# Head-centred values and initial states in a bidirectional RWKV step: the mean of the chunk norm leaves the latent scans

## The chip, the cores and the metric

One core of a Trainium2 chip. The metric is the device time of one execution of the whole kernel in microseconds (us), as the median of several runs. Engines: TensorE (PE; its weight loads, PEld, are recorded apart), VectorE (DVE), ScalarE (ACT), GpSimd (POOL), and SyncE (SP), which issues DMAs.

## The reference, cut to what matters

One layer of a bidirectional hybrid backbone on 1024 latent and 128 context tokens, model width 1024. A projection `z = xn @ w_in` gives receptances, keys, values and gates. Sixteen heads of 64 run an RWKV-7 recurrence forward and backward, the outputs of both directions are added, and each head's output is normalised over its 64 value dimensions:

```python
def step(S, inp):
    r_t, w_t, k_t, v_t, a_t, b_t = inp
    sa = jnp.einsum('bhvk,bhk->bhv', S, a_t)
    S = S * w_t[:, :, None, :] + sa[..., None] * b_t[:, :, None, :] + v_t[..., None] * k_t[:, :, None, :]
    return S, jnp.einsum('bhvk,bhk->bhv', S, r_t)
...
wkv = ys[0] + ys[1]
mu = jnp.mean(wkv, axis=-1, keepdims=True)
var = jnp.mean(jnp.square(wkv - mu), axis=-1, keepdims=True)
ln = ((wkv - mu) * lax.rsqrt(var + LNX_EPS)).reshape(B, T, D_RWKV) * p['lnx_w'] + p['lnx_b']
```

The output is linear in the values `v` and the initial state `S0` along the value dimension. So if each token's `v` and each column of `S0` have zero mean over the 64 value dimensions of a head, `wkv` has it too, and `mu` is zero. The final states of the context scan are an output of their own and must not be centred. The bonus term uses the uncentred `v`. Around the recurrence stand a gated short convolution, an output projection and a squared-ReLU MLP.

## The kernel before, in words

Heads are worked on in 8 pairs (128 rows: two heads of 64). The kernel has three stages.

**Projections** (the dense loop over `p` in every engine's function). For each pair TensorE fills PSUM banks in a fixed order, held by the class `Fills` (L104): first the low-rank products `w0, w1, a0, a1`, then `AFTER` (L99): `k, r, v, ks, cc, ch, vt, cb, g, za, bon, zb`. Each name is three fills of 384 tokens (`g` is six: for each third of the tokens one bank per head). Eight banks go round: fill n uses the bank of fill n - 8 and waits until that was emptied (`Fills.freed`, `free_bank`). `BY_DVE` (L101) names the fills that VectorE empties (`ch`, `cb`, `bon`); ScalarE empties the others. `vt` is the transpose of the values (`vf`) to token-major form; ScalarE copies it to `vn` (L1616), from where SP stores it to `v_d` (L674). VectorE's order in a pair is: decay sums, the substitution for the pair before, key scaling, the operands, then the product of `ch` with `cc` (L2071), the convolution (L2076 to L2083), the eviction of `cb` (L2088) and that of `bon` (L2093). `g` is the diagonal product of TensorE (`diagonal`, L1075), which asks for both of its banks before each third. ScalarE rounds a weight block for the high part (`split_high`), POOL forms the low part (L847), and SP loads blocks four ahead into a ring.

**Scans.** 72 units: for each pair, chunks j = 0 to 7 of 128 latent tokens (forward chunk j together with backward chunk 7 - j) and one context chunk (j = 8), which starts from a zero state. Step s of each engine's loop holds a fixed list of work for several units in flight: TensorE turns and inverts (`turn`, `left`, `right`), forms the grams of unit s + 4 and does the serial products of unit s (`ur_state`, `serial_ur`, `serial_u`, `serial_s`, `serial_y`). ScalarE moves `ur` (L1651) and `up` (L1655) to SBUF; VectorE masks the grams (L2108), updates the states (L2157), and adds the second half of `y` (L2168) for j = 4 to 7, ScalarE the first half for the other j. `first_state(p)` (L2129) makes a pair's initial states by two products at the step j = 8 of the pair before. One chunk is finished in each step from s = 5 on (`finals`, L177): TensorE takes the head sums of `y` with a block of ones (`mean`, L1296), VectorE subtracts (`centred`, L2180), ScalarE squares (L1675), TensorE sums the squares (`variance`) and forms the gate product (`gate`), ScalarE takes the root, VectorE the reciprocal (L2184), TensorE spreads it, and VectorE scales (`scaled`, L2189 to L2196). 67 chunks are finished in the loop and five in a tail behind it (`TAIL`, L187).

**Dense stage.** Output projections and MLP as 11 products of 7 block products each (L1411), not touched.

Of the kernel before, what the change touches and what calls it, by code (L numbers as in the profile page):

```python
# [22 lines left out]
P = 128  # L23
# [4 lines left out]
G = 3  # L28
# [69 lines left out]
LOW_RANK = [(x + str(d), cg) for x in "wa" for cg in range(G) for d in range(2)]  # L98
AFTER = ["k", "r", "v", "ks", "cc", "ch", "vt", "cb", "g", "za", "bon", "zb"]  # L99
DIAGONAL = [(f"g{h}", cg) for cg in range(G) for h in range(2)]  # L100
BY_DVE = ("ch", "cb", "bon")  # L101


class Fills:  # L104
# [59 lines left out]
def y_seen(u):  # L164

    p, j = divmod(u, NC)
    if y_by_act(j):
        return "ya_ok", 5 * p + (j + 1 if j < NC_LAT else 5)
    return "yd_ok", 4 * p + j - 3
# [7 lines left out]
def finals(s):  # L177

    p, j = divmod(s, NC)
    if s < 0 or s >= UNITS:  # L180
        return []
    if j > 4:
        return [(p, FIN_ORDER[j - 5], NC * p + j - 5)]
    return [(p - 1, FIN_ORDER[4 + j], NC * (p - 1) + 4 + j)] if p else []
# [88 lines left out]
def flow_step(nc, xs, xp, wblocks, wquads, pack, packl, vecs, csil_in, consts, gfin, y_out, yp_out, st_out):  # L273
    ctx = ExitStack()
    with ctx:
# [20 lines left out]
        def sb(st, name, shape, dt=F32):  # L296
            return st.enter_context(nc.sbuf_tensor(name, shape, dt))
# [41 lines left out]
        pk = sb(dense, "pk", [P, PK])  # L339
        half = sb(dense, "half", [P, 6])  # L340
        mid = sb(dense, "mid", [P, 2, NC])
        dense.close()
        rounded = ExitStack()
        sb(rounded, "under_cv", [P, (KT + 5) * T])
# [44 lines left out]
        state = [[sb(sc, f"state{d}{q}", [P, HD]) for q in range(2)] for d in range(2)]  # L389
        mrow = sb(sc, "mrow", [P, MG])  # L390
        fstd = sb(sc, "fstd", [P, 5, 2])
        fbon, fsq = (sb(sc, n, [P, 5, C]) for n in ("fbon", "fsq"))
        tok = [sb(sc, f"tok{q}", [P, 2, 4, HD]) for q in range(TOKS)]
        pl = [sb(sc, f"pl{q}", [P, PL]) for q in range(2)]
# [573 lines left out]
        def _(pe):  # L968
# [325 lines left out]
                return banks[(0, 4, 2)[k] + i // 4][:, (i % 4) * P:(i % 4 + 1) * P]  # L1294

            def mean(p, c, n):  # L1296
                name, seen = y_seen(NC * p + (max(c, NC_LAT - 1 - c) if c < NC_LAT else NC_LAT))
                pe.wait_ge(S[name], seen)
                if 0 < n < TAIL[0][2]:
                    pe.wait_ge(S["xa_ok"], n)  # L1300
                for hs in halves_of:
                    ins = mm(place(n, 0)[hs, :], bones[hs, hs], yf[p % 2][hs, c * C:(c + 1) * C], True, True)
                ins.then_inc(S["mu_full"], 1)
# [18 lines left out]

            def gate(p, c, n):
                pe.wait_ge(S[f"pl_in{p % 2}"], 16 * (p // 2 + 1))
                if n < TAIL[0][2]:
                    pe.wait_ge(S["yc_ok"], n + 1)
                for b in halves_of:
                    ins = mm(place(n, 2)[b, :], pl[p % 2][:, PL_G2 + b.start:PL_G2 + b.stop], gl[:, c * C:(c + 1) * C], True, True)
                ins.then_inc(S["gate_full"], 1)
# [7 lines left out]
            def modulation_turned(g):  # L1337
                pe.wait_ge(S["mrow_ok"], g + 1)
                if g:
                    pe.wait_ge(S["yc_ok"], finals(NC * g + 3)[0][2] + 1)  # L1340
                for b in range(4):
                    ins = mm(banks[2][:, 3 * P + 2 * b:3 * P + 2 * b + 2], mrow[:, b * P:(b + 1) * P], sel[:], True, True)
                ins.then_inc(S["mt_full"], 1)
# [144 lines left out]
        def _(act):  # L1488
# [41 lines left out]
            def empty(p, name, out, func, **kw):  # L1530
                for cg in range(G):
                    act.wait_ge(S["fill_full"], FL.full(p, name, cg))
                    A(out(cg), banks[FL.bank(p, name, cg)][:, :GN], func, **kw).then_inc(ev["A"], 1)
# [33 lines left out]
            for p in range(PAIRS):  # L1567
                act.wait_ge(S["half_ok"], p + 1)
                for kind in "wa":
                    if p:  # L1570
                        for d in range(2):
                            act.wait_ge(S[f"so_{'ar0' if kind == 'w' else 'bk0'}{d}"], 16 * p)
                    for name, cg in LOW_RANK:
                        if name[0] == kind:
                            d = int(name[1])
                            dst = (ar0 if kind == "w" else bk0)[d]
                            b = d if kind == "w" else 2 + d
                            act.wait_ge(S["fill_full"], FL.full(p, name, cg))
                            A(dst[:, cols(cg)], banks[FL.bank(p, name, cg)][:, :GN], ACT.Tanh, scale=0.5, bias=half[:, b:b + 1]).then_inc(ev["A"], 1)
                for d in range(2):  # L1580
                    own(p, f"w{d}")
                    A(ar0[d][:], ar0[d][:], ACT.Copy, scale=-0.5 * DECAY, bias=-0.5 * DECAY).then_inc(S["logw_ok"], 1)
                if p:
                    act.wait_ge(S["op_ok"], 8 * p)
                    act.wait_ge(S["prod_ok"], p)
                    act.wait_ge(S["g_out"], 32 * p)
                empty(p, "k", lambda cg: kt[:, cols(cg)], ACT.Copy)
                next_split(p, "k")
                own(p, "k")
                A(kd[1][:], kt[:], ACT.Square, scale=pk[:, PK_VEC + V_KK:PK_VEC + V_KK + 1]).then_inc(S["kksq_ok"], 1)  # L1590
                act.wait_ge(S["kksq_ok"], p + 1)
                if p:
                    act.wait_ge(S["gb_out"], 16 * p)
                A(cv_r[:], kd[1][:], ACT.Copy).then_inc(S["parts_ok"], 1)
                k_factor(p, 0)
                decays(p, 0)
                empty(p, "r", lambda cg: rt[:, cols(cg)], ACT.Copy)
                next_split(p, "r")
                decays(p, 1)
                if p:  # L1600
                    act.wait_ge(S["so_f"], 16 * p)
                empty(p, "v", lambda cg: vf[:, cols(cg)], ACT.Copy)
                next_split(p, "v")
                if p:
                    act.wait_ge(S["inv_ok"], p)
                empty(p, "ks", lambda cg: kk[:, cols(cg)], ACT.Sqrt)
                k_factor(p, 1)
                if p:
                    act.wait_ge(S["ga_out"], 16 * p)
                empty(p, "cc", lambda cg: cct[:, cols(cg)], ACT.Copy)  # L1610
                next_split(p, "cc")
                next_split(p, "ch")
                if p:
                    act.wait_ge(S["so_v"], 16 * p)
                    act.wait_ge(S["x_out"], 64 * Q * p)
                empty(p, "vt", lambda cg: vn[:, cols(cg)], ACT.Copy)  # L1616
                next_split(p, "cb")
                act.wait_ge(S["prod_ok"], p + 1)
                A(kd_r[1][:], kd[0][:], ACT.Copy).then_inc(S["parts_ok"], 1)
                for name, cg in DIAGONAL:  # L1620
                    act.wait_ge(S["fill_full"], FL.full(p, name, cg))
                    A((kt, rt)[int(name[1])][:, cols(cg)], banks[FL.bank(p, name, cg)][:, :GN], ACT.Copy).then_inc(ev["A"], 1)
                act.wait_ge(S["conv_ok"], p + 1)
                empty(p, "za", lambda cg: cct[:, cols(cg)], ACT.Tanh, scale=0.5)
                next_split(p, "za")
                act.wait_ge(S["xb_out"], 16 * p + 16)
                empty(p, "zb", lambda cg: cv[:, cols(cg)], ACT.Tanh, scale=0.5)
                next_split(p, "zb")
# [42 lines left out]
                return banks[2][:, 4 * P - 2:4 * P] if i < 0 else ser[:, 1, 2 * i:2 * i + 2]  # L1671

            def squares_of(p, c, n):
                act.wait_ge(S["yc_ok"], n + 1)
                A(fsq[:, n % 5, :], yf[p % 2][:, c * C:(c + 1) * C], ACT.Square).then_inc(S["ysq_ok"], 1)  # L1675

            def deviation(p, c, n):
# [193 lines left out]
        def _(dve):  # L1871
# [141 lines left out]
            def substitution(p, some=range(SUB - 1), ways=(0, 1)):  # L2013
# [9 lines left out]
                for x in some:  # L2023
# [8 lines left out]
                    for d in ways:  # L2032
# [6 lines left out]
                        else:  # L2039
                            ch.step(ins)  # L2040
                            done[d] = ch.n

            halves(0)
            dve.wait_ge(ev["A"], FL.emptied("l", 2)[1])
            V.tensor_scalar(gl[:], gl[:], 0.5, 0.5, mul, add).then_inc(S["gl_ok"], 1)
            for p in range(PAIRS):
# [22 lines left out]
                for cg in range(G):  # L2069
                    x = full(p, "ch", cg)  # L2070
                    V.tensor_tensor(cct[:, cols(cg)], x, cct[:, cols(cg)], mul).then_inc(ev["D"], 1)  # L2071
                filled(p, "ch")
                if p:
                    dve.wait_ge(S["gb_out"], 16 * p)
# [53 lines left out]

            def first_state(p):  # L2129
                dve.wait_ge(S[f"pl_in{p % 2}"], 16 * (p // 2 + 1))  # L2130
                for d in range(2):
                    c = chunk(d, 0)
                    V.tensor_scalar(state[d][0][:], pl[p % 2][:, PL_ST + d * HD:PL_ST + (d + 1) * HD], emid[:, p, d, c:c + 1], None, mul).then_inc(S["s_ok"], 1)

            def carried(u):

# [38 lines left out]
                return banks[(0, 4, 2)[k] + i // 4][:, (i % 4) * P:(i % 4 + 1) * P]  # L2175

            def centred(p, c, n):
                dve.wait_ge(S["mu_full"], n + 1)
                y = yf[p % 2][:, c * C:(c + 1) * C]
                stt(y, place(n, 0), -1.0 / HD, y, mul, add).then_inc(S["yc_ok"], 1)  # L2180

# [52 lines left out]
            for x in finals(UNITS - 1):  # L2234
                reciprocal(*x)
                scaled(*x)
            dve.wait_ge(S["mu_full"], UNITS)
            for x in TAIL:
                centred(*x)
            for x in TAIL:  # L2240
# [324 lines left out]
```

## Time and profile before

| | |
|---|---|
| median of 3 runs | 2705.92 us (2702.68 to 2709.07) |
| the profiled execution | 2705.67 us, of which the span from first to last instruction is 2703.6 us |
| mean granted clock of TensorE | 0.985 of full speed |
| TensorE busy | 2580.1 us (95%) |
| VectorE busy | 1852.0 us (68%) |
| ScalarE busy | 1080.2 us (40%) |
| POOL busy | 1175.8 us (43%) |

Projections last from about 100 to 1020 us of the span, the scans to about 1640 us. Times in the rows are microseconds from the start of the span unless they are marked ns. A row of the timeline has start, length, engine, line, operation and tiles (out<-in), and in brackets the time for which the engine stood before it and what ended that time. Busy shares are averages over stages; L970 is a helper through which nearly all matmuls are issued, so they are told apart by their tiles.

### The profile page before, as it was taken

How to read it: one execution, taken by the hardware profiler on the slowest of the kernel's cores; microseconds unless marked ns; L12 is line 12 of the kernel's file. 1: busy time of each engine (PE TensorE's matmuls, PEld its weight loads, DVE VectorE, ACT ScalarE, POOL GpSimd, SP SyncE). 2: the span in 40 equal slices, each digit the busy share in tenths (PEclk: the TensorE clock that was granted, in tenths of full speed). 3: DMA queues.
4: the chain of work that ended last, by engine and by line, in shares of the span. 5: the costliest groups of instructions: out<-in, count | busy, mean ns of one | idle time of the engine just before them, and what ended most of it. 6: DMA issues, size and time to landing. Idle time of an engine off the chain costs nothing.

```text
span 2703.6 us, 68164 instructions
## 1 busy us (share of the span) xinstructions
PE 2580.1 (95%) x28864; PEld 2430.1 (90%) x28864; DVE 1852.0 (68%) x3010; ACT 1080.2 (40%) x1978; POOL 1175.8 (43%) x1154
## 2 busy tenths in 40 slices
PE   4899999999999998999999997999799999999998
PEld 3899999999999996788878887999799999999998
DVE  3464665846748464787766666799778679678686
ACT  3434243342433422433333343443453353443534
POOL 1323222322223224555555544656446556565662
PEclk8999999999999999999999999999899999999999
DMA  8333425435254363444454456454223232333231
GB/s 323 106 110 109 144 69 181 125 97 158 62 174 128 94 193 108 131 143 144 138 154 137 139 160 195 131 175 105 63 63 79 81 101 70 79 84 102 65 79 71
DMA packets 282412, 329.15 MB, mean 122 GB/s; under 512 B 76288, under 2 KB 215936, under 8 KB 273536
## 3 DMA queue, kind: packets, MB, share of 16 engines
q1 hardware_dynamic: 274448, 278.66, 33.2%
q0 software_dynamic: 5904, 39.32, 6.9%
q10 hardware_dynamic: 1760, 6.82, 0.6%
q8 instruction: 231, 3.78, 0.6%
q14 instruction: 69, 0.57, 0.1%
HBM read 221.83 MB, written 91.36 MB: 116 GB/s over the span
## 4 chain that ended last, share of the span: by engine, by line
PE 85%; DVE 7%; issue 2%; DMA 2%; ACT 2%; SPq 1%; POOL 0%; DVEq 0%; ACTq 0%; POOLq 0%
PE ser L970 18%; PE gbank L970 13%; PE bank L970 11%; PE inv L970 11%; PE gbank L1411 8%; PE inv L1411 8%; PE ser L1411 7%; PE bank L1411 7%; DVE a_sum L2298 1%; DMA ring<-in_wblocks 1%; PE inv L1172 1%; PE bank L1155 1%; DVE a_sum L2302 1%; DVE a_sum L2306 1%; DVE a_lo L2272 1%
## 5 line engine op out<-in xcount | busy, mean ns | idle before, releaser
L952 POOL TENSOR_TENSOR w_lo<-raw_w,w_hi 128x512 fp32r<-128x512 f32 x264 | 425.3, 1624 | 370.2 <-ACT w_hi L1747 370.1
L847 POOL TENSOR_TENSOR wsp<-ring,wsp 128x1024 fp32r<-128x1024 f32 x67 | 210.8, 3146 | 670.7 <-ACT wsp L1513 670.7
L1747 ACT ACTIVATE w_hi<-raw_w 128x512 fp32r<-128x512 f32 x264 | 165.1, 632 | 262.5 <-PE ser L1411 98.4
L970 PE MATMUL ser<-xn_hi,wsp 128*128 128x384 f32 x816 | 217.7, 340 | 6.1 <-POOL xn_lo L853 6.1
L1411 PE MATMUL gbank<-a_hi,w_hi 128*128 128x288 f32 x616 | 185.7, 302 | 30.6 <-POOL w_lo L952 14.6
L970 PE MATMUL gbank<-xn_hi,wsp 128*128 128x384 f32 x800 | 213.0, 339 | 1.1 <-issue 1.1
L970 PE MATMUL bank<-xn_hi,wsp 128*128 128x384 f32 x800 | 211.1, 338 | 2.2 <-POOL wsp L847 2.2
L970 PE MATMUL inv<-xn_hi,wsp 128*128 128x384 f32 x800 | 211.3, 338 | 0.5 <-issue 0.5
L2108 DVE TENSOR_TENSOR gmat<-gbank,gmask 128x1024 f32<-128x1024 f32 x144 | 175.6, 1219 | 49.8 <-PE gbank L970 49.0
L1733 ACT ACTIVATE a_hi<-a_sum 128x1152 fp32r<-128x1152 f32 x88 | 103.1, 1173 | 224.6 <-DVE a_sum L2306 78.0
L970 PE MATMUL gbank<-ub 64*64 64x128 f32 (+1 forms) x3456 | 178.4, 310 | 9.5 <-DVE gmat L2108 5.6
L1411 PE MATMUL gbank<-a_hi,w_lo 128*128 128x288 f32 x616 | 184.7, 300 | 0.0
L1411 PE MATMUL gbank<-a_lo,w_hi 128*128 128x288 f32 x616 | 184.4, 299 | 0.0
L1411 PE MATMUL inv<-a_hi,w_lo 128*128 128x288 f32 x616 | 183.9, 299 | 0.0
L1411 PE MATMUL inv<-a_hi,w_hi 128*128 128x288 f32 x616 | 183.7, 298 | 0.0
L1411 PE MATMUL inv<-a_lo,w_hi 128*128 128x288 f32 x616 | 183.6, 298 | 0.0
L1411 PE MATMUL ser<-a_hi,w_hi 128*128 128x288 f32 x616 | 181.6, 295 | 1.5 <-ACT r L1786 1.5
L1411 PE MATMUL bank<-a_hi,w_lo 128*128 128x288 f32 x616 | 181.8, 295 | 0.0
L1411 PE MATMUL ser<-a_hi,w_lo 128*128 128x288 f32 x616 | 181.7, 295 | 0.0
L1411 PE MATMUL ser<-a_lo,w_hi 128*128 128x288 f32 x616 | 181.4, 294 | 0.0
L1411 PE MATMUL bank<-a_lo,w_hi 128*128 128x288 f32 x616 | 181.4, 294 | 0.0
L1411 PE MATMUL bank<-a_hi,w_hi 128*128 128x288 f32 x616 | 181.3, 294 | 0.0
(398 smaller groups left out, 7534.7 us busy)
## 6 DMA issues: line engine op xcount, KB each, us to landing
ring<-in_wblocks SPq DMA_DIRECT2D x107, 512.0 KB, 4.8
ub<-op_d SPq DMA_DIRECT2D x144, 256.0 KB, 2.8
raw_w<-in_wquads SPq DMA_DIRECT2D x33, 1024.0 KB, 4.8
raw_w<-in_wquads POOLq DMA_DIRECT2D x22, 1024.0 KB, 8.8
op_d<-ar SPq DMA_DIRECT2D x32, 576.0 KB, 5.4
op_d<-bk SPq DMA_DIRECT2D x32, 576.0 KB, 6.2
raw_w<-in_wquads SPq DMA_DIRECT2D x44, 256.0 KB, 3.3
raw_w<-zsum POOLq DMA_DIRECT2D x11, 1024.0 KB, 12.3
```

The costliest lines, as they stand in the source:

```text
L847: GT(wsp[s % 2][1][:], ring[(N_ADA_RING + s) % RING][:], wsp[s % 2][0][:].bitcast(F32), ALU.subtract).then_inc(S["wsplit_lo"], 1)
L952: GT(w_lo[n % 4][:], src, w_hi[n % 4][:].bitcast(F32), ALU.subtract).then_inc(S["wl_ok"], 1)
L970: return nc.tensor.matmul(out, lhsT, rhs, start=start, stop=stop)
L1155: ins = nc.tensor.transpose(banks[3][:, y * P:(y + 1) * P], ub[v % LOADS][:, y // 2, 2 + y % 2, :], ident[:])
L1172: ins = nc.tensor.transpose(inv[:, 0, x * P:(x + 1) * P], xt[:, place_of(v), :, :].rearrange("p h t -> p (h t)"), ident[:])
L1411: return nc.tensor.matmul(out, lhsT, rhs, start=start, stop=stop, skip_group_check=True)
L1733: A(a_hi[:, places2(q, j), :], src, ACT.Copy).then_inc(S["ah_ok"], 1)
L1747: A(w_hi[s][:], raw_of(op)[:, m, :].rearrange("p (k c) -> p k c", k=KH), ACT.Copy).then_inc(S["wh_ok"], 1)
L2108: V.tensor_tensor(gmat[v % SETS][:, d, :, :, :].rearrange("p h x t -> p h (x t)"), gbank[:, :, :], gmask[:, d:d + 1, :].to_broadcast([P, 2 ...
L2272: V.tensor_tensor(a_lo[:, places2(q, j), :], src, a_hi[:, places2(q, j), :].bitcast(F32), sub).then_inc(S["al_ok"], 1)
L2298: ch.step(V.tensor_tensor(o[j], a11[j], a12[j], sub))
L2302: ch.step(V.tensor_tensor(o[j], o[j], a22[j], add))
```

## The change

The values leave the projection stage centred per head for the latent tokens, the initial latent states are centred, and the scans skip the mean product and the subtraction for latent chunks. Context chunks keep both. The waits on the centred output are moved to what now comes last (`y_seen`, `xa_ok`).

```diff
-BY_DVE = ("ch", "cb", "bon")
+BY_DVE = ("ch", "vt", "cb", "bon")
...
+        vmean = sb(dense, "vmean", [P, G, 2 * G])
+        smean = sb(sc, "smean", [P, 2])
...
             def mean(p, c, n):
-                name, seen = y_seen(NC * p + (max(c, NC_LAT - 1 - c) if c < NC_LAT else NC_LAT))
-                pe.wait_ge(S[name], seen)
+                if c == NC_LAT:
+                    name, seen = y_seen(NC * p + NC_LAT)
+                    pe.wait_ge(S[name], seen)
                 if 0 < n < TAIL[0][2]:
                     pe.wait_ge(S["xa_ok"], n)
+                if c < NC_LAT:
+                    return
...
             def gate(p, c, n):
                 pe.wait_ge(S[f"pl_in{p % 2}"], 16 * (p // 2 + 1))
-                if n < TAIL[0][2]:
-                    pe.wait_ge(S["yc_ok"], n + 1)
+                if n < TAIL[0][2] and c == NC_LAT:
+                    pe.wait_ge(S["yc_ok"], p + 1)
...
                 if g:
-                    pe.wait_ge(S["yc_ok"], finals(NC * g + 3)[0][2] + 1)
+                    pe.wait_ge(S["xa_ok"], finals(NC * g + 3)[0][2])
...
                 next_split(p, "ch")
-                if p:
-                    act.wait_ge(S["so_v"], 16 * p)
-                    act.wait_ge(S["x_out"], 64 * Q * p)
-                empty(p, "vt", lambda cg: vn[:, cols(cg)], ACT.Copy)
                 next_split(p, "cb")
...
             def squares_of(p, c, n):
-                act.wait_ge(S["yc_ok"], n + 1)
+                if c < NC_LAT:
+                    name, seen = y_seen(NC * p + max(c, NC_LAT - 1 - c))
+                    act.wait_ge(S[name], seen)
+                else:
+                    act.wait_ge(S["yc_ok"], p + 1)
...
+            def value_tokens(p):
+
+                n = [2 * G] * (G - 1) + [2 * G - 2]
+                for cg in range(G):
+                    x = full(p, "vt", cg).rearrange("p (g v) -> p g v", v=HD)
+                    ch.step(V.tensor_reduce(vmean[:, cg, 0:n[cg]], x[:, 0:n[cg], :], mybir.AxisListType.X, add))
+                ch.settle()
+                if p:
+                    dve.wait_ge(S["so_v"], 16 * p)
+                    dve.wait_ge(S["x_out"], 64 * Q * p)
+                for cg in range(G):
+                    x = full(p, "vt", cg).rearrange("p (g v) -> p g v", v=HD)
+                    stt(vn[:, cols(cg)].rearrange("p (g v) -> p g v", v=HD), bc(vmean[:, cg, :], HD), -1.0 / HD, x, mul, add).then_inc(ev["D"], 1)
...
                     V.tensor_tensor(cct[:, cols(cg)], x, cct[:, cols(cg)], mul).then_inc(ev["D"], 1)
+                value_tokens(p)
                 filled(p, "ch")
...
             def first_state(p):
                 dve.wait_ge(S[f"pl_in{p % 2}"], 16 * (p // 2 + 1))
+                s0 = pl[p % 2][:, PL_ST:PL_ST + 2 * HD]
+                ch.step(V.tensor_reduce(smean[:], s0.rearrange("p (d v) -> p d v", v=HD), mybir.AxisListType.X, add))
+                ch.settle()
+                ch.step(V.tensor_scalar(smean[:], smean[:], -1.0 / HD, None, mul))
+                ch.settle()
                 for d in range(2):
                     c = chunk(d, 0)
-                    V.tensor_scalar(state[d][0][:], pl[p % 2][:, PL_ST + d * HD:PL_ST + (d + 1) * HD], emid[:, p, d, c:c + 1], None, mul).then_inc(S["s_ok"], 1)
+                    V.tensor_scalar(state[d][0][:], s0[:, d * HD:(d + 1) * HD], smean[:, d:d + 1], emid[:, p, d, c:c + 1], add, mul).then_inc(S["s_ok"], 1)
...
             def centred(p, c, n):
-                dve.wait_ge(S["mu_full"], n + 1)
+                if c < NC_LAT:
+                    return
+                dve.wait_ge(S["mu_full"], p + 1)
```

## Rows read from the trace of the kernel before

**Rows 1.** Windows of projections and scans: length; busy PE, PEld, DVE, ACT, POOL; PEclk, DMA.

```profile
300.00:500.00 200.00, 200.00 (x1396) 194.83 (x1395) 115.66 (x232) 83.12 (x128) 58.11 (x19) 1.00 0.42 128
1200.00:1300.00 100.00, 99.81 (x2471) 80.90 (x2468) 72.20 (x176) 38.41 (x105) 50.97 (x110) 1.00 0.45 134
```

**Rows 2.** The page's chain that ended last, shares by engine.

```profile
PE 85%; DVE 7%; issue 2%; DMA 2%; ACT 2%; SPq 1%; POOL 0%; DVEq 0%; ACTq 0%; POOLq 0%
```

**Rows 3.** Groups by line: busy us, mean ns of one | idle before, releaser.

```profile
L970 PE MATMUL bank<-yf,bones 64*64 64x128 f32 x268 | 26.8, 270 | 1.4 <-DVE yf L2196 0.9 <-issue 0.5
...
L2180 DVE SCALAR_TENSOR_TENSOR yf<-bank,yf 128x128 f32<-128x128 f32 x67 | 19.5, 291 | 14.2 <-PE bank L970 13.0
...
L2184 DVE RECIPROCAL fstd<-fstd 128x2 f32<-128x2 f32 x72 | 11.4, 159 | 15.0 <-ACT fstd L1681 14.9
```

**Rows 4.** Timeline of two scan steps, weight loads, and ScalarE in the second.

```profile
1045.22 0.55 PEld L970 LDWEIGHTS ser<-ur,tt 128*64 128x64 f32 x16 [0.17 <-issue]
1046.78 0.20 PEld L970 LDWEIGHTS ser<-up,tok 128*64 128x64 f32 x4 [0.39 <-ACT up L1655]
...
1242.86 0.55 PEld L970 LDWEIGHTS ser<-ur,tt 128*64 128x64 f32 x16 [0.17 <-issue]
...
1244.63 0.20 PEld L970 LDWEIGHTS ser<-up,tok 128*64 128x64 f32 x4 [0.17 <-issue]
...
1243.59 0.38 ACT L1655 ACTIVATE up<-ser 128x256 f32<-128x256 f32 x1 [0.98 <-PE ser L970]
```

**Rows 5.** Timeline of VectorE in one pair's projections.

```profile
418.51 1.02 DVE L2071 TENSOR_TENSOR cct<-gbank,cct 128x384 f32<-128x384 f32 x2
419.44 0.55 DVE L2071 TENSOR_TENSOR cct<-bank,cct 128x384 f32<-128x384 f32 x1
420.02 0.82 DVE L2076 TENSOR_SCALAR cv<-cct,pk 128x1152 f32<-128x1152 f32 x1
...
424.07 1.02 DVE L2088 TENSOR_TENSOR cv<-ser,cv 128x384 f32<-128x384 f32 x2
```

**Rows 6.** Timeline of the weight loads in the same pair.

```profile
419.11 0.19 PEld L970 LDWEIGHTS gbank<-xn_hi,wsp 128*128 128x128 f32 x1 [0.28 <-DVE cct L2071]
...
424.88 0.14 PEld L970 LDWEIGHTS ser<-ar,bk 64*64 64x64 f32 x2
```

**Rows 7.** Timeline of SyncE's DMA queue in the same pair.

```profile
379.89 5.78 SPq L626 DMA_DIRECT2D x_d<-vn  x15
...
418.42 1.25 SPq L674 DMA_DIRECT2D v_d<-vn  x1
```

**Rows 8.** Timeline at a pair boundary of the scans, VectorE and weight loads.

```profile
1261.32 1.22 DVE L2108 TENSOR_TENSOR gmat<-gbank,gmask 128x1024 f32<-128x1024 f32 x1
...
1264.65 0.21 PEld L970 LDWEIGHTS inv<-xtb,gmat 64*64 64x64 f32 x8 [0.17 <-POOL lm L878]
```

**Rows 9.** Gaps of TensorE: timeline, windows (PE busy, PEclk, DMA), last-ending chain.

```profile
1904.96 0.19 PEld L1411 LDWEIGHTS gbank<-a_hi,w_hi 128*128 128x128 f32 x1 [1.85 <-DVE r L2377]
...
1906.00:1908.00 2.00, 2.00 (x18) 1.00 0.59 201
...
1702.08 0.19 PEld L1411 LDWEIGHTS gbank<-a_hi,w_hi 128*128 128x128 f32 x1 [3.19 <-ACT r L1761]
...
1704.00:1706.00 2.00, 2.00 (x10) 0.50 0.00 0
...
1702.11 4.95 PE gbank L1411 x24
1707.05 3.18 PE bank L1411 x24
...
1040.67 1.16 PEld L970 LDWEIGHTS gbank<-ub 64*64 64x64 f32 x24 [2.27 <-DMA vb<-v_d]
...
1305.60 0.65 PEld L970 LDWEIGHTS gbank<-ub 64*64 64x64 f32 x24
```

**Rows 10.** Timeline of the weight loads, a step with j = 7.

```profile
1247.42 0.32 PEld L970 LDWEIGHTS ser<-state,ub 64*64 64x64 f32 x16 [0.27 <-DVE yf L2168]
```

More of the change, by code:

```diff
@@ L2041, in substitution @@
                             done[d] = ch.n
+            def value_tokens(p):
[10 more added lines that the diff above has]
+                    stt(vn[:, cols(cg)].rearrange("p (g v) -> p g v", v=HD), bc(vmean[:, cg, :], HD), -1.0 / HD, x, mul, add).then_inc(ev["D"], 1)
             halves(0)
+            ch.step(V.memset(vmean[:, G - 1, 2 * G - 2:2 * G], 0.0))
             dve.wait_ge(ev["A"], FL.emptied("l", 2)[1])
@@ L2236, in _ @@
                 scaled(*x)
-            dve.wait_ge(S["mu_full"], UNITS)
+            dve.wait_ge(S["mu_full"], PAIRS)
             for x in TAIL:
```

## The prediction

> **What bounds the kernel now.** I read the windows by stage first, to see which engine is full in which stage [rows 1]: TensorE is busy for all 200 of 200 us in the projections and for 99.8 of 100 us in the scans, VectorE for 58% and 72%. The chain that ended last agrees [rows 2]: 85% of the span is TensorE. So VectorE and ScalarE count only where TensorE waits for them, and a busy TensorE record may still hide a wait (matmul ends are modelled); therefore the places themselves are read in the timeline of TensorE's weight loads, which shows when its queue stands.
>
> **Part 1, removed: the mean product of 64 latent chunks.** Sixty lie inside the scans (67 chunks are finished in the loop, seven of them context chunks, which keep it), four in the tail. The product's group is 26.8 us busy for 67 chunks, 0.40 us each, and the centring 0.29 us on VectorE [rows 3]. But what a step gains is read from two steps that differ by just this [rows 4]: with the mean, 1.77 us pass from the first weight load of `serial_u` (1242.86) to that of `serial_s` (1244.63); in pair 0, where no chunk is being finished yet, 1.56 us (1045.22 to 1046.78). The difference is 0.21 us, half the busy time, because the matmuls of the gram before it still fill the array. `serial_s` also waits for ScalarE's `up`, which ends at 1243.97 (1243.59 + 0.38), 1.11 us after `serial_u` began: it stays just off the path. Gain 60 x 0.21 = 12.6 us. Bounds: 0, and 60 x 0.40 = 24 us. The centring on VectorE is worth nothing: the states behind it wait for TensorE. The four tail chunks save at most 4 x 0.29 = 1.2 us and are taken at nothing; the gates there wait for an earlier chunk's last VectorE step. The square on ScalarE may start earlier, which nobody waits for.
>
> **Part 2, moved: the token-major values go from ScalarE (3 copies a pair, on an engine 42% busy: worth nothing) to VectorE as 3 reductions, a wait for them, and 3 subtractions.** Queued behind them on VectorE are the convolution and then the eviction of `cb`; and the eviction of `cb`'s first group is what TensorE waits for. Eight PSUM banks go round: the third group of the diagonal product `g` takes the bank of the first group of `cb` (fill 14 of the list against fill 6). How tight this is shows in one pair [rows 5]: VectorE evicts `ch` from 418.51 to 419.99, starts the convolution at 420.02 and the `cb` evictions at 424.07, so the first is done at 424.62 (0.55 us). TensorE begins the third group of `g` at 424.88 [rows 6]: 0.26 us of slack. The same kind of wait exists already: TensorE stood 0.28 us for the first `ch` eviction (ended 419.06, load at 419.11, so 0.05 us for the signal).
>
> The added work: instructions on 128x384 PSUM follow each other every 0.47 us ((419.44 - 418.51)/2) [rows 5]. From 419.91 on: two reductions at 0.47, the third (256 elements) at its full 0.41 (0.55 less 128 elements at the 1.0 ns that lie between the 384-element row [rows 5] and the 128-element one [rows 3]), 0.04 for the wait, three subtractions at 0.47: the convolution starts at 422.71 instead of 420.02, 2.69 us later. The first `cb` bank is free at 427.31, plus 0.05 for the signal: TensorE starts the third group at 427.36 instead of 424.88, a stall of 2.48 us. Nothing gives it back: TensorE is full before and behind, and VectorE's next work in the pair is anchored to TensorE's fills. 8 x 2.48 = 19.8 us lost. No row shows a reduction. If it cost nothing, the stall would be 2.48 - 1.25 = 1.2 us (9.8 us in all; some of the wait stays); if it ran at half the rate, 3.84 us (30.7 us). I take the rate of the nearest row, the `ch` eviction.
>
> The Trainium skill, page "VectorE: DVE Perf Modes", section "The DRAIN you can't avoid", says that a VectorE instruction starts only when the pipe of the one before it is empty. The `ch` evictions here overlap by 0.08 us, so the trace disagrees; by the rule the six would take about 3.2 us and the loss would be 24 us instead of 19.8. Its "Rules for kernel authors" call `tensor_reduce` the slowest VectorE instruction, with one element per cycle: a rule against this change, which no row here shows.
>
> The waits for the older `v_d` and `x_d` transfers now stand on VectorE; the last `x_d` store is issued by 385.7, 35 us before, and `v_d` a pair before [rows 7], so they cost nothing. SP waits for the `vt` eviction, so the `v_d` store (418.42) goes out some 4.3 us later, and with it the weight load queued behind it; `xb_d`, `pk` and `g_d` go some 2.7 us later. The weight ring is loaded four blocks ahead, and the queue is idle between; without this cover the 4.3 us would stand once a pair.
>
> **Part 3, added: the centred initial state.** At seven pair boundaries VectorE does a reduction over 128 elements, a two-element scale and two waits: 0.29 [rows 3] + 0.16 + 2 x 0.04 = 0.53 us, before the mask of the next gram (1261.32) [rows 8]. Behind that mask are POOL's `lm` (0.17 us waited for at 1264.65) and the next gram. With some 0.13 us of slack: 7 x 0.4 = 2.8 us lost. Bounds 0 and 3.7.
>
> **Part 4, the clock.** A stop of 2.5 us may cost more than itself. A gap of 1.85 us in dense work left the granted clock at 1.00; a gap of 3.19 us was followed by 0.50 (1.2 GHz), and the group of 24 matmuls behind it took 4.95 instead of 3.18 us; a gap of 2.27 us in sparse work (1040.67) lies on the same side, since the loads behind it took 1.16 us where the same 24 take 0.65 [rows 9]. So one fall costs 1.77 us; between 0 and 8 of the new stops (0 to 14.2 us) cause one. The new gap lies between the rows, about half-way; I take three, 5.3 us. The Trainium skill, page "TensorE: Matmul & The Clock Gate", section "What's actually happening", says that the throttled state is the default and that activity releases it; that makes a new stop a candidate each time, and by it alone the time would be the dear case below.
>
> **The sum.** -12.6 + 19.8 + 2.8 + 5.3 = +15.3 us. The profiled execution took 2705.7 us (span 2703.6), the median of three runs is 2705.9; so 2721 us. A measurement of this kernel can tell about 0.2% (5.4 us) from no change.
>
> **Rivals.**
> - Faster, about 2696 us. A scan step is set by VectorE's chain and not by TensorE, so that the removed centring takes with it the 0.27 us for which TensorE waits for VectorE's `yf` [rows 10] in the four last latent steps of a pair (32 x 0.27 = 8.6 us), besides the full 0.40 us (24 us). 32.6 against 19.8 + 2.8 gives -10 us. It decides from 0.47 us a chunk on ((22.6 + 5.4)/60). For it: TensorE does wait there. Against it: [rows 4] have the step without a mean, and it is 0.21 shorter. Chance 0.09.
> - No difference, about 2706 us. The reductions cost next to nothing and no clock falls: 9.8 + 2.8 - 12.6 = 0. For it: no reduction is in the trace; against it: 384 elements are read however it is done. Chance 0.14.
> - The dear case, about 2731 us. The clock falls at all or nearly all eight stops: 2721 - 5.3 + 14.2 = 2730, with a slower reduction more. Chance 0.15.
> - The forecast: a stall of 2 to 3 us in each pair, with up to five falls of the clock, 2711 to 2726 us. Chance 0.62.
> That the mean isn't really removed can be left out: the diff returns before its matmuls.
>
> **How the numbers follow.** The likeliest is 2721. The range goes from 2707 to 2731: from the upper part of the no-difference case, over the forecast, to the dear case without its tail. Slower by over 0.2%: 0.62 + 0.15 = 0.77; within 0.2%: 0.14; faster: 0.09.
>
> **What would show it.** In the projections: three reductions and three subtractions between the evictions of `ch` and the convolution, about 2.7 us together; a gap of about 2.5 us in the weight loads before the third group of `g`, released by VectorE's `cv`, eight times; a granted clock of 0.50 behind some of them. A pair should last 2.5 us and more longer. In the scans: a step shorter by 0.21 us, with 1.56 us from `serial_u` to `serial_s`; a pair of nine steps shorter by about 1.7 us less 0.4 at its boundary. I am wrong if TensorE has no such gap, if the gap is under 1.2 us, or if a step shrinks by 0.4 us or more.

## The result, and the profile after

| | before | after |
|---|---|---|
| median of 4 runs each, same chip | 2706.19 us (2702.68 to 2709.07) | 2755.26 us (2750.86 to 2758.60) |
| span of the profiled execution | 2703.6 us | 2756.6 us |
| mean granted clock | 0.985 | 0.976 |
| up to the first scan step (ScalarE's first `ur`) | 1043.75 us | 1106.07 us |
| from there to the last of the 72 steps | 580.20 us | 572.38 us |
| behind it | 1079.65 us | 1078.15 us |

The changed kernel is 1.8% slower: ratio 1.0181, 95% interval 1.0160 to 1.0202. The forecast was 2721 us, its range ended at 2731: the direction was right, the size was not. The last three lines of the table, each worked out from the timeline of ScalarE, say where the time went: +62.3 us in the projections, -7.8 in the scans, -1.5 behind them. The scans gave 7.8 of the 9.8 us that were forecast; the projections lost two and a half times the forecast (19.8 + 5.3 = 25.1 us).

The windows answer to [rows 1] (same columns). TensorE, full in 200 of 200 us before, now is busy for 187; the scans hardly differ.

```profile
300.00:500.00 200.00, 186.83 (x1303) 181.31 (x1302) 120.79 (x187) 67.72 (x103) 49.36 (x16) 0.97 0.44 133
1200.00:1300.00 100.00, 99.20 (x2453) 79.65 (x2449) 80.48 (x204) 38.30 (x105) 51.74 (x111) 1.00 0.47 139
```

The waits of the weight loads between 100 and 1060 us (total, times, longest) name the loss. There are eight stops, two on each of four banks, 53.4 us in all, each 6.7 us long. All are released by VectorE's `cv`, as forecast; the forecast length was 2.48 us.

```profile
PEld inv L972 <- DVE cv L2109: 13.4, 2, 6.7
PEld gbank L972 <- DVE cv L2109: 13.4, 2, 6.7
PEld bank L972 <- DVE cv L2109: 13.3, 2, 6.7
PEld ser L972 <- DVE cv L2109: 13.3, 2, 6.7
```

Why 6.7 is read from VectorE's timeline of one pair (it answers to [rows 5]):

```profile
435.86 1.02 DVE L2091 TENSOR_TENSOR cct<-gbank,cct 128x384 f32<-128x384 f32 x2
436.79 0.55 DVE L2091 TENSOR_TENSOR cct<-bank,cct 128x384 f32<-128x384 f32 x1
437.26 0.55 DVE L2053 TENSOR_REDUCE vmean<-bank 128x6 f32<-128x384 f32 x1
437.72 0.88 DVE L2053 TENSOR_REDUCE vmean<-inv 128x6 f32<-128x384 f32 x2
438.63 0.55 DVE L2060 SCALAR_TENSOR_TENSOR vn<-vmean,bank 128x384 f32<-128x384 f32 x1
439.11 1.01 DVE L2060 SCALAR_TENSOR_TENSOR vn<-vmean,inv 128x384 f32<-128x384 f32 x2
440.03 0.81 DVE L2097 TENSOR_SCALAR cv<-cct,pk 128x1152 f32<-128x1152 f32 x1
440.88 1.53 DVE L2100 SCALAR_TENSOR_TENSOR cv<-cct,pk,cv 128x1008 f32<-128x1008 f32 x2
442.45 3.24 DVE L2103 SCALAR_TENSOR_TENSOR cv<-cct,pk,cv 128x1008 f32<-128x1008 f32 x1
445.61 2.69 DVE L2104 SCALAR_TENSOR_TENSOR cv<-cct,pk,cv 128x127 f32<-128x127 f32 x1
448.39 1.02 DVE L2109 TENSOR_TENSOR cv<-ser,cv 128x384 f32<-128x384 f32 x2
```

The six new instructions are just what was forecast. From the start of the last `ch` eviction to the start of the convolution 3.24 us pass (436.79 to 440.03) against 0.58 before (419.44 to 420.02): 2.66 us added, 2.69 forecast. But the convolution itself, 4.05 us before (420.02 to 424.07), now takes 8.36 us (440.03 to 448.39). Two of its instructions have grown: the third tap (the shift by one token the other way, over the latent tokens) goes from 1.27 to 3.24 us, and its short partner over the context chunk from 0.35 to 2.69 us. It is so in every pair, as the groups by form show (x8, mean ns 3237 and 2691; 1269 and 346 before).

Beside them stands POOL. Its timeline, first before, then after:

```profile
411.01 3.52 POOL L847 TENSOR_TENSOR wsp<-ring,wsp 128x1024 fp32r<-128x1024 f32 x1 [9.11 <-ACT wsp L1513]
424.78 2.39 POOL L847 TENSOR_TENSOR wsp<-ring,wsp 128x1024 fp32r<-128x1024 f32 x1 [10.25 <-ACT wsp L1513]
427.13 2.67 POOL L859 TENSOR_TENSOR kd_r<-kd,kd_r 128x1152 fp32r<-128x1152 f32 x1
```

```profile
442.16 2.46 POOL L849 TENSOR_TENSOR wsp<-ring,wsp 128x1024 fp32r<-128x1024 f32 x1 [10.28 <-ACT wsp L1518]
444.58 3.57 POOL L861 TENSOR_TENSOR kd_r<-kd,kd_r 128x1152 fp32r<-128x1152 f32 x1
```

Before, the convolution ended at 423.98 and POOL began at 424.78: 0.80 us apart. Pushed back by 2.66 us, the convolution's last two instructions overlap POOL's two, and the times read as turns taken one instruction at a time. The third tap (issued at 442.45) ends 1.07 us behind the end of POOL's weight block (444.62). POOL's `kd_r`, begun at 444.58, ends at 448.15, 2.46 us behind the end of the third tap (445.69), where it alone takes 2.67. The short instruction (346 ns alone) ends at 448.30, 0.15 us behind `kd_r`. All of these read two operands in SBUF. The reductions and subtractions, which read PSUM, kept their 0.47 us spacing, but POOL stood idle beside them (its wait of 10.28 us ends at 442.16), so this row doesn't tell whether POOL could slow them.

The Trainium skill, page "SBUF — State Buffer", section "Who interferes with whom", has this: a VectorE instruction with two SBUF inputs contends with a GpSimd instruction that reads SBUF, over a port pair locked for whole instructions. The trace agrees in size and in order. The prediction did not use it, though [rows 5] lie next to a case of it in the trace of before: of two like products, the one that began ahead of POOL's 3.52 us block kept its 1.35 us, and the one issued while that block ran took 3.43 us. It ended at 415.74, 1.21 us behind the block (411.01 + 3.52 = 414.53).

```profile
410.93 1.35 DVE L2003 TENSOR_TENSOR ar<-kk,ar 128x1152 f32<-128x1152 f32 x1
412.31 3.43 DVE L2006 TENSOR_TENSOR bk<-kd,bk 128x1152 f32<-128x1152 f32 x1
```

The weight loads of the same pair answer to [rows 6]; the windows behind the stop (PE busy, PEclk, DMA share, GB/s) show the second loss.

```profile
440.85 0.14 PEld L972 LDWEIGHTS gbank<-ar,bk 64*64 64x64 f32 x2 [0.25 <-issue]
449.06 0.21 PEld L972 LDWEIGHTS inv<-ar,bk 64*64 64x64 f32 x2 [6.72 <-DVE cv L2109]
```

```profile
442.00:444.00 2.00, 0.48 (x35) 1.00 0.99 279
444.00:446.00 2.00, 0.00 (x0) 0.90 0.39 147
446.00:448.00 2.00, 0.00 (x0) 0.50 0.02 8
450.00:451.00 1.00, 1.00 (x27) 0.50 0.31 124
453.00:454.00 1.00, 1.00 (x8) 1.00 1.06 240
...
574.13:575.13 1.00, 1.00 (x5) 0.50 0.85 238
```

The granted clock falls to 0.50 (1.2 GHz) while TensorE stands and comes back after it has resumed. So it is behind all eight stops, but not for the same time: here it is back 3.3 us after TensorE resumes (449.06 to 452.4), behind the fourth stop only after 6.2 us (569.13 to 575.3; last row), and the eight stretches together last 37.6 us. At half the clock half of that is lost, 18.8 us (an estimate from these lengths). The lengths of the pairs agree: the pair behind the sixth stop, with 3.2 us of low clock, lasts 120.0 us, the one behind the fourth 121.2. SyncE's `v_d` store ([rows 7]) went out at 440.14, ahead of the stop and with no wait of TensorE behind it. The chain of [rows 2] is of no help after: its shares sum to 60%, so it breaks off in the middle and can't be set beside the one before.

In the scans a step without its mean has the 1.56 us between `serial_u` and `serial_s` that [rows 4] promised:

```profile
1295.70 0.55 PEld L972 LDWEIGHTS ser<-ur,tt 128*64 128x64 f32 x16 [0.17 <-issue]
1297.26 0.20 PEld L972 LDWEIGHTS ser<-up,tok 128*64 128x64 f32 x4 [0.39 <-issue]
```

Undisturbed latent steps are 0.21 us shorter (from one `ur` to the next, 7.94 us become 7.73 and 7.30 become 7.09). The wait for `yf` of [rows 10] stays as it was, and at the pair boundary ([rows 8]) VectorE's three steps for the state stand ahead of the mask of the next gram:

```profile
1307.88 0.33 PEld L972 LDWEIGHTS ser<-state,ub 64*64 64x64 f32 x16 [0.27 <-DVE yf L2194]
...
1321.65 0.28 DVE L2153 TENSOR_REDUCE smean<-pl 128x2 f32<-128x128 f32 x1
1321.96 0.17 DVE L2155 TENSOR_SCALAR smean<-smean 128x2 f32<-128x2 f32 x1
1322.17 0.54 DVE L2159 TENSOR_SCALAR state<-pl,smean,emid 128x64 f32<-128x64 f32 x2
1322.62 1.22 DVE L2129 TENSOR_TENSOR gmat<-gbank,gmask 128x1024 f32<-128x1024 f32 x1
```

The step over the boundary, also without its mean, lasts 8.15 instead of 7.83 us: the initial state costs 0.32 + 0.21 = 0.53 us there, nearly what lies between 1321.65 and 1322.17 (0.52).

### The profile page after: what moved, and what is told of

It reads as the page before. It is cut to its first block, busy times and chain, and to the rows that moved or that the text cites. A ratio compares the mean times of both kernels' runs of the same rounds, so it can differ in the third digit from the quotient of the medians.

```text
span 2756.6 us, 67518 instructions
## 1 busy us (share of the span) xinstructions
PE 2584.8 (94%) x28608; PEld 2429.5 (88%) x28608; DVE 1892.6 (69%) x3011; ACT 1072.0 (39%) x1954; POOL 1183.0 (43%) x1154
## 4 chain that ended last, share of the span: by engine, by line
PE 50%; DVE 7%; ACT 1%; issue 1%; DMA 1%; SPq 0%; POOL 0%; DVEq 0%; ACTq 0%; POOLq 0%
PE ser L972 9%; PE gbank L1416 8%; PE inv L1416 7%; PE ser L1416 7%; PE bank L1416 7%; PE gbank L972 5%; PE inv L972 3%; PE bank L972 2%; DVE a_sum L2326 1%; PE inv L1174 1%; DVE a_sum L2330 1%; PE bank L1157 1%; DVE a_sum L2334 1%; DVE a_lo L2300 1%; DVE r L2405 1%
## 6 DMA issues: line engine op xcount, KB each, us to landing
raw_w<-zsum POOLq DMA_DIRECT2D x11, 1024.0 KB, 12.3
```

## The experiments

Two theories. **A**: the extra stop is contention with POOL, called forth by the delay, and the clock follows the stop. **B**: VectorE's added work stretches the pair whatever POOL does, by a queue or a wait that the prediction missed. First the two halves of the change were run apart.

**The values alone.** The kernel before with `value_tokens` on VectorE and without ScalarE's copy of `vt`; the scans keep their means.

```diff
-BY_DVE = ("ch", "cb", "bon")
+BY_DVE = ("ch", "vt", "cb", "bon")
...
+                value_tokens(p)
                 filled(p, "ch")
```

> The kernel before with the projection part of the change alone (values centred on VectorE, token-major copy taken from ScalarE); the scans keep the mean product and the centring for every chunk, initial states stay as they were. Theory (the loss is all in the projections: each pair stops TensorE for 6.7 us, and the clock falls behind each stop): 2706 + 64 = 2770 us, seven to ten us above the changed kernel. Rival (a good part of the loss is in the scans or in what the two parts do together): clearly below 2760 us.

Measured: 2765.6 us, ratio 1.0221 (1.0204 to 1.0238); eight stops of 6.72 to 6.75 us, and the clock at 0.50 behind all. The scans take 579.89 us, as before (580.20). The whole loss is made by this half.

**The scans alone.** The changed kernel with the copy of `vt` back on ScalarE. It leaves out the centring of the values, so its norm lacks the mean for latent tokens and that output is not the reference's.

```diff
+                empty(p, "vt", lambda cg: vn[:, cols(cg)], ACT.Copy)
...
-                value_tokens(p)
```

> The changed kernel with the token-major copy back on ScalarE and the values not centred, so the output lacks the mean of the chunk norm for latent tokens; the scan part and the centred initial states stay. Theory: the scans gain 0.21 us for each of 60 chunks and lose some 0.5 us at seven boundaries: 9 us less than before, 2697 us. By the busy time of the removed products (0.40 us each) it would be 2686 us; if the scan part had any hidden loss, 2706 us or more.

Measured: 2692.55 us, ratio 0.9952 (0.9937 to 0.9967). The scans take 571.08 us, 9.1 less than before: 60 x 0.21 less 7 x 0.53 is 8.9. The removed means are worth what the rows said. The two halves add up: +60.8 and -12.3 us give +48.5, against +49.1 for both together. But the 12.3 us are more than the scans give: in the profiled execution the first `ur` also comes 4.8 us earlier (1038.95), though the edit leaves the projections as they were before. A part of that is found under the sum below.

**POOL held back.** The changed kernel, but POOL begins the low part of the weight block only when the convolution is done. VectorE's work and order stay the same, so that theory B expects no change.

```diff
+                p, b = divmod(s - 2 - N_LORA, PAIR_BLOCKS)
+                if p >= 0 and STREAM[b] == "cb":
+                    pool.wait_ge(S["conv_ok"], p + 1)
                 split_low(s)
-                p, b = divmod(s - 2 - N_LORA, PAIR_BLOCKS)
```

> The changed kernel, with one wait more on POOL: it starts the low part of the block that comes with cb only when VectorE's convolution is done. Theory (the convolution, 2.7 us late, runs beside POOL's two instructions and is slowed by them, 4.2 us a pair): the third and fourth convolution instructions go back to 1.27 and 0.35 us, the stop falls from 6.7 to 2.5 us: 2755 - 34 = 2721 us, and down to 2708 us if the clock no longer falls behind the shorter stops. Rival (they are slow for another reason, transfers or TensorE's clock): no change, 2755 us, or more, since POOL comes later.

Measured: 2712.64 us, ratio to the kernel before 1.0025 (1.0011 to 1.0040). The timelines of VectorE, POOL and the weight loads in the same pair:

```profile
431.28 1.27 DVE L2105 SCALAR_TENSOR_TENSOR cv<-cct,pk,cv 128x1008 f32<-128x1008 f32 x1
432.47 0.35 DVE L2106 SCALAR_TENSOR_TENSOR cv<-cct,pk,cv 128x127 f32<-128x127 f32 x1
...
432.89 2.38 POOL L849 TENSOR_TENSOR wsp<-ring,wsp 128x1024 fp32r<-128x1024 f32 x1 [12.18 <-DVE cv L2106]
...
433.58 0.17 PEld L974 LDWEIGHTS inv<-ar,bk 64*64 64x64 f32 x2 [2.43 <-DVE cv L2111]
```

Both VectorE instructions are back at their old lengths and the stop is 2.43 us; the difference to 6.72 us is 4.29 us, and the two instructions had grown by 4.31. One added wait on POOL, which adds no work and takes none away, leaves 7.8 us of loss where there were 49.1 (each against the kernel before, run beside it): 41 us come back. That settles A against B.

This kernel shows the clock too. Its eight stops are all 2.35 to 2.43 us long; behind five the granted clock falls to 0.50, behind three it stays at 1.00. Windows behind one of each:

```profile
434.00:436.00 2.00, 2.00 (x47) 1.00 0.43 169
...
549.00:551.00 2.00, 2.00 (x8) 0.50 0.99 304
```

A pair (from its first `ch` stop to the next pair's) lasts 115.1 us where the clock falls and 113.5 where it does not: a fall costs 1.6 us (1.4 by the same comparison in the next kernel). In both kernels the clock stays low for 3.4 us, nearly all of it behind the stop, so the price is about half of that time. It can't be carried to the longer stops of the changed kernel, where the clock stays low for 3.2 to 6.2 us after TensorE resumes. The profiled execution of this kernel (2719.8 us) was the slowest of nine.

**The convolution first.** The changed kernel with the values centred behind the convolution, ahead of the `cb` evictions.

```diff
-                value_tokens(p)
                 filled(p, "ch")
...
                 dve.wait_ge(S["conv_ok"], p + 1)
+                value_tokens(p)
                 for cg in range(G):
                     x = full(p, "cb", cg)
```

> The changed kernel with the same six instructions behind the convolution instead of ahead of it. Theory (two-input VectorE instructions with both inputs in SBUF are slowed while POOL works, those that read PSUM are not): the convolution takes 4.0 us again, the six instructions 2.8 us, the stop is 2.5 us: as e3, 2708 to 2721 us. Rival A (POOL slows any VectorE instruction): the six take 6 us and the time stays near 2755 us. Rival B (VectorE's added work is the whole cost, in whatever order): 2755 us too.

Measured: 2713.23 us, ratio 1.0035 (1.0023 to 1.0046). Now it is the new instructions that run beside POOL, and they keep their times:

```profile
431.66 0.88 DVE L2053 TENSOR_REDUCE vmean<-inv 128x6 f32<-128x384 f32 x2
432.57 0.56 DVE L2060 SCALAR_TENSOR_TENSOR vn<-vmean,bank 128x384 f32<-128x384 f32 x1
...
431.90 2.35 POOL L849 TENSOR_TENSOR wsp<-ring,wsp 128x1024 fp32r<-128x1024 f32 x1 [10.25 <-ACT wsp L1518]
...
433.71 0.17 PEld L972 LDWEIGHTS bank<-ar,bk 64*64 64x64 f32 x2 [2.32 <-DVE vn L2060]
```

So company of POOL alone is not enough: it is instructions with two operands in SBUF that are held up. The stop is 2.25 to 2.33 us, its releaser is another (`vn`), and the clock again falls behind five of eight.

**Centred in SBUF, behind the evictions.** ScalarE copies `vt` out of PSUM as before; VectorE centres the copy in place when `cb` has been evicted, and the store of `v_d` waits for that.

```diff
...
+                filled(p, "vt")
+                x = vn[:, 0:LAT].rearrange("p (g v) -> p g v", v=HD)
+                ch.step(V.tensor_reduce(vmean[:], x, mybir.AxisListType.X, add))
+                ch.settle()
+                stt(x, bc(vmean[:], HD), -1.0 / HD, x, mul, add).then_inc(S["mrow1_ok"], 1)
...
```

> The changed kernel, but ScalarE copies vt to SBUF as before, and VectorE takes the mean of vn and subtracts it there, behind the eviction of cb, where it has 13 us of idle time; the store of v_d goes out after it. Theory (only the place of the added VectorE work cost time, not its amount): no stop of TensorE before the third group of g, projections as before, the gain of the scans is kept: as with the scan part alone, about 2693 us, 12 us below the kernel before. Rival (values centred on VectorE cost time in the projections wherever they stand, by POOL's low parts or by the later store of v_d): between 2700 and 2721 us.

Measured: 2686.03 us, ratio 0.9933 (0.9918 to 0.9948), 7 us below what was expected (the last bullet on why the prediction was wrong comes back to this). The work is no smaller, and POOL even pays for it, but TensorE doesn't wait:

```profile
424.32 1.21 DVE L2101 TENSOR_REDUCE vmean<-vn 128x16 f32<-128x1024 f32 x1
425.57 1.57 DVE L2103 SCALAR_TENSOR_TENSOR vn<-vmean,vn 128x1024 f32<-128x1024 f32 x1
...
423.65 2.40 POOL L850 TENSOR_TENSOR wsp<-ring,wsp 128x1024 fp32r<-128x1024 f32 x1 [10.27 <-ACT wsp L1519]
426.00 3.67 POOL L862 TENSOR_TENSOR kd_r<-kd,kd_r 128x1152 fp32r<-128x1152 f32 x1
```

POOL's `kd_r` (2.67 us alone) ends 2.53 us behind the subtraction: the same turn-taking, here with POOL as the one held up. The reduction, which reads one operand from SBUF, began and ended while POOL's weight block ran (424.32 to 425.53), and that block kept its 2.40 us: one operand in SBUF takes no turn. The weight loads have no stop at `g`.

**And the mean of the initial state early.** The last kernel, with the reduction and scale of the next pair's state issued one step before the boundary.

```diff
...
+                if there(s) and j == NC_LAT - 1 and p + 1 < PAIRS:
+                    state_mean(p + 1)
```

> e5, and the head means of the next pair's initial states are formed one step earlier, in the step j = 7, where VectorE is idle. Theory: the 0.5 us that the step from j = 8 to j = 0 gained at seven boundaries go again, so 3 us below e5, about 2690 us. Rival: the longer boundary comes from something else (the state products with two scalars, the transfers), then no difference to e5.

Measured: 2683.82 us, ratio 0.9930 (0.9914 to 0.9946). The boundary step goes from 8.15 to 7.62 us, so the 0.53 us come back in full; the two medians (2686.03 and 2683.82, where 3 us were expected) lie too close to be told apart, so the trace alone shows it. This version beats both kernels: 20 us under the kernel before (2704.14 us beside it), some 70 under the changed one.

## Why the prediction was wrong

- **Part 1, the removed means: right.** 0.21 us a step was forecast and measured, 12.6 us for 60 steps. The "faster" rival, which needed 0.47 us a chunk, is out.
- **Part 2, the added work: its first half right, its last wrong.** Reductions at 0.55 us (0.41 for the short one) every 0.47 us: the rate of an eviction was the right choice. The rival in which they cost nothing is out. The Trainium skill, page "VectorE: DVE Perf Modes", section "Rules for kernel authors", calls `tensor_reduce` the slowest of VectorE's operations; for this size the trace disagrees, since it takes the 0.55 us of the eviction. The prediction's reading of that page's section "The DRAIN you can't avoid" was too strict. It made 3.2 us of the six, but the section adds that an instruction that is not held starts earlier, and the trace has 2.77 us (437.26 to 440.03). With the contention taken out, the stop is 2.43 us against 2.48. **The step that failed** is the next one: "The first `cb` bank is free at 427.31" moved the convolution by 2.69 us and kept its old length of 4.05 us. That length had a cover, the 0.80 us between its end and POOL's start, which the delay used up. The step should have asked what runs on POOL in the new place of each instruction. In its place the runs showed a convolution of 8.36 us, turn by turn with POOL, and a stop of 6.7 us. Cost: 8 x 4.3 = 34 us, plus the clock (part 4).
- **Part 2, "Nothing gives it back": not quite.** In the kernel before, TensorE stood in the later pairs for nothing that the profile shows (queue waits, for short); one such row:

```profile
877.23 0.19 PEld L970 LDWEIGHTS bank<-xn_lo,wsp 128*128 128x128 f32 x1 [2.08 <-issue]
```

  Between 200 and 1012 us there are four above 0.4 us, 6.1 us together (6.3 with the scans alone, 1.8 and 2.3 in the last two kernels). The four kernels with a stop in each pair have none. That a stop lets TensorE's queue catch up would fit; no run tested it.
- **Part 3, the initial state: 0.4 forecast, 0.53 measured,** the full length of its instructions: the assumed 0.13 us of slack isn't there. 0.9 us in all.
- **Part 4, the clock: 3 falls of 8 were forecast, 5.3 us.** With stops of about the forecast length it is 5 of 8 at 1.6 us each (1.77 forecast), 8 us; with stops of 6.7 us it is 8 of 8, and since the clock stays low for longer, 18.8 us or 2.35 each. Even the dear bound (14.2 us) was too low for that.
- **The sum after the fact.** Stops 53.4, low clock 18.8, queue waits gone -6.1: 66.1 us against +62.3 measured ahead of the scans. Scans: -12.6 + 3.7 = -8.9 against -7.8. Of the 3.8 us too much, 1.0 lies ahead of the first pair (TensorE's wait for `gl` ends at 117.17 instead of 118.17); the rest and the 1.1 us of the scans were not traced. Single groups of 48 weight loads take 8.48 us in the projections of both main kernels in most places (42 times before, 40 times after; 8.32 us three times and once). In each of the six experiments 21 to 24 of them take 8.32 us. The cause stays open. It makes some 4 us (24 x 0.16) that each experiment has in its favour against both main kernels: far less than the 41 us of POOL's wait, but most of the 4.8 us by which the first `ur` came earlier with the scans alone.
- **The range.** Its dear end let all eight clocks fall but not the stop grow. Without the contention the result is 2712.6 us (POOL held back), inside it. The gain of the last two kernels (18 and 20 us) is also more than the scans explain (7.8 and 13.0 us in the profiled executions). Some 4 us are the queue waits above and some 4 us the shorter groups; why either changed stays open.

## What to carry to other kernels

An instruction that is pushed back keeps its length only if its new neighbours are as kind as the old ones: before a delay is summed, lay the other engines' timelines over the new place, and look in the old trace for an instruction of the same shape that is longer than its twins. Where VectorE and POOL instructions each read two operands from SBUF, they took turns by whole instructions here, so order them so that the one off the critical path waits; one wait on POOL was worth 41 us. When a clock fall is priced, measure how long the clock stays low behind that very stop, since the price of a shorter stop doesn't carry over. Work whose result is stored and read much later belongs behind the evictions that TensorE waits for, even if it needs one more pass.

## What the runs showed of the hardware that was not expected

- A VectorE instruction of 346 ns took 2691 ns, because it stood behind a POOL instruction of 2.67 us; here the neighbour's length set the price and not its own.
- Stops of TensorE of nearly one length (2.25 to 2.43 us, the same work ahead) lowered the granted clock five times and left it alone three times, in the same three pairs (third, fifth, seventh) in the profiled executions of both kernels with such stops. What tells these pairs apart was not found.
- Behind stops of one length (6.67 to 6.72 us) the clock stayed at 0.50 for 3.2 to 6.2 us after TensorE resumed in the changed kernel, and for 3.5 to 4.0 us in the kernel with the values alone. What sets this was not found.
- A reduction of 128x384 from PSUM to 128x6 takes 0.55 us, as long as a product that writes all 384 columns.
